# A two-layer encoder on one core: ten channel-major projections in half-width units with high and low part in one matmul, and memory in four parts

## What is computed

```python
h = rms_norm(x, mix_norm_g[i])
proj = h @ w_in[i]
da_q, da_k, da_v, s_z, s_xbc, s_dt, xa_q, gates = split_cols(proj, IN_SIZES)
y_da = diff_attention(da_q, da_k, da_v, lam, lambda_init, da_subln_g[i])
y_ssm = mamba2_bidir(s_z, s_xbc, s_dt, conv_w, conv_b, dt_bias, A_log, D, ssm_norm_g)   # convolution, silu, scans
y_xa = mem_cross_attention(xa_q, rms_norm(mem, mem_norm_g[i]), w_mem_kv[i])
x = x + (g0 * (y_da @ wb_da) + g1 * (y_ssm @ wb_ssm) + g2 * (y_xa @ wb_xa)) @ w_out[i]
gate, up = split_cols(rms_norm(x, ffn_norm_g[i]) @ w_ffn_in[i], (FFN_HIDDEN, FFN_HIDDEN))
x = x + (silu(gate) * up) @ w_ffn_out[i]
```

## Time and profile before

| what | value |
|---|---|
| median of 3 runs | 1413.91 us (1413.8 to 1414.85) |
| the profiled execution | 1414.03 us, its span 1412.3 us |
| TensorE busy | 1393.9 us (99%) |
| VectorE busy | 918.5 us (65%) |
| ScalarE busy | 885.6 us (63%) |
| GpSimd busy | 322.3 us (23%) |
| HBM traffic | 250.18 MB read, 178 GB/s over the span |

### The profile page before, as it was taken

How to read it: one execution, slowest core, us unless ns; L and a number is a source line. 1 busy time by engine, 2 the same in 40 slices (tenths; PEclk the granted TensorE clock), 3 DMA queues, 4 the chain that set the end, 5 groups by cost and what they waited for, 6 DMA issues and landing times.

```text
span 1412.3 us, 22092 instructions
## 1 busy us (share of the span) xinstructions
PE 1393.9 (99%) x8215; PEld 1222.1 (87%) x8231; DVE 918.5 (65%) x1243; ACT 885.6 (63%) x1432; POOL 322.3 (23%) x161
## 2 busy tenths in 40 slices
PE   7999999999999999999999999999999999999998
PEld 7899898888888889888899998988888888888886
DVE  5468575897998445554454775768889874555532
ACT  6576667986756446556445765778777464565543
POOL 0410000011023444444414000001110244344442
PEclk9999999999999999999999999999999999999999
DMA  7655445567665555666555555455756555566663
GB/s 250 189 172 174 124 134 166 159 199 200 203 194 178 183 177 180 192 192 218 185 184 170 165 152 147 133 174 143 223 190 230 179 166 192 164 194 182 192 194 119
DMA packets 157893, 252.80 MB, mean 179 GB/s; under 512 B 12649, under 2 KB 59355, under 8 KB 157787
## 3 DMA queue, kind: packets, MB, share of 16 engines
q1 hardware_dynamic: 156624, 249.50, 57.7%
q10 hardware_dynamic: 1163, 1.89, 0.4%
HBM read 250.18 MB, written 1.18 MB: 178 GB/s over the span
## 4 chain that ended last, share of the span: by engine, by line
PE 88%; DVE 4%; ACT 3%; DVEq 2%; DMA 1%; issue 1%; ACTq 0%; SPq 0%
PE PS L617 70%; PE S L617 14%; DVE wL L1367 1%; ACT wH L974 1%; PE S L624 1%; ACT scr L1135 1%; DVEq L1706 1%; DVE actLf L1635 1%; DMA w_raw<-in_w_in_dram 1%; DMA regA<-in_mem_dram 0%; PE S L936 0%; PE S L871 0%; DVEq L1637 0%; PE S L842 0%; DVE regA L1707 0%
## 5 line engine op out<-in xcount | busy, mean ns | idle before, releaser
L974 ACT CAST wH<-w_raw 128x1024 fp32r<-128x1024 f32 x440 | 457.6, 1043 | 457.4 <-PE PS L617 318.9
L1367 DVE TENSOR_TENSOR wL<-w_raw,wH 128x1024 fp32r<-128x1024 f32 (+1 forms) x328 | 416.0, 1273 | 341.9 <-ACT wH L974 323.3
L1302 POOL TENSOR_TENSOR wL<-w_raw,wH 128x1024 fp32r<-128x1024 f32 (+1 forms) x112 | 270.1, 2411 | 416.1 <-ACT wH L974 416.1
L617 PE MATMUL PS<-hHL,wH 128*128 128x256 f32 (+2 forms) x2016 | 314.8, 303 | 0.0
L617 PEld LDWEIGHTS PS<-hHL,wH 128*128 128x128 f32 (+1 forms) x2016 | 266.4, 190 | 10.9 <-issue 2.7
L617 PE MATMUL PS<-wH,actH 128*128 128x512 f32 x560 | 223.5, 399 | 0.0
L617 PE MATMUL PS<-wH,actL 128*128 128x512 f32 x560 | 218.4, 390 | 0.0
L617 PE MATMUL PS<-wH,hHL 128*128 128x512 f32 x768 | 200.7, 403 | 0.0
L617 PE MATMUL PS<-hHL,wL 128*128 128x256 f32 (+1 forms) x1168 | 172.0, 282 | 0.0
L617 PEld LDWEIGHTS PS<-wH,hHL 128*128 128x128 f32 x768 | 140.1, 188 | 33.3 <-issue 6.5
L617 PEld LDWEIGHTS PS<-hHL,wL 128*128 128x128 f32 (+1 forms) x1168 | 158.4, 190 | 6.2
(11 more groups left out here) (252 smaller groups left out, 1573.9 us busy)
## 6 DMA issues: line engine op xcount, KB each, us to landing
w_raw<-in_w_in_dram SPq DMA_DIRECT2D x192, 512.0 KB
w_raw<-in_w_ffn_in_dram SPq DMA_DIRECT2D x176, 256.0 KB
w_raw<-in_w_branch_dram SPq DMA_DIRECT2D x64, 512.0 KB
w_raw<-in_w_ffn_out_dram SPq DMA_DIRECT2D x44, 512.0 KB
w_raw<-in_w_mem_kv_dram SPq DMA_DIRECT2D x32, 512.0 KB
regA<-cs_rows SPq DMA_DIRECT2D x64, 256.0 KB, 4.9
w_raw<-in_w_out_dram SPq DMA_DIRECT2D x16, 512.0 KB
regA<-in_mem_dram SPq DMA_DIRECT2D x2, 768.0 KB, 7.0
```

What stands on the lines that cost most here:

```text
L617: return nc.tensor.matmul(o, l, r, start=first, stop=last, skip_group_check=True)
L974: nc.scalar.copy(wH[:, slot].rearrange("p k c -> p (k c)")[:, q], raw[:, slot].rearrange("p k c -> p (k c)")[:, q]).then_inc(h_done[slot], 1)
L1302: nc.gpsimd.tensor_tensor(wL[:, slot].rearrange("p k c -> p (k c)")[:, q], raw[:, slot].rearrange("p k c -> p (k c)")[:, q], wH[:, slot].r ...
L1367: v.tensor_tensor(wL[:, slot].rearrange("p k c -> p (k c)")[:, q], raw[:, slot].rearrange("p k c -> p (k c)")[:, q], wH[:, slot].rearrange ...
```

## The change

Ten groups per layer (xbc4, xq0, xbc5, xq1, xbc0, q0, k0, xbc1, q1, k1) get a layout W. A unit of theirs is 4 K tiles by 256 columns, so two units fill one pair of banks with half of the group: 2 tiles of 128 channels, each 512 columns wide, high and low activations side by side. The high weights take 8 matmuls of 512 columns and the low weights 8 of 256. The two halves of a bank have to be added: ScalarE copies the low half out (`wide_corr`, 512 columns), and VectorE adds it to the high half (`wide_sum`, 512 columns), which frees the pair. Such a group is two fills of PSUM, two units each. For xbc groups the middle tap now reads from `cin` (`conv_mid`) after the sum.

Memory comes in four parts of 256 columns between the first weight loads. The third and fourth block are transposed just ahead of unit 1's and unit 2's matmuls. VectorE copies the transposed blocks into `keep`, SyncE stores them to DRAM, and layer 1 reads them back and needs no transpose or squares. Parameter loads go from ScalarE's queue to SyncE's, behind the loads of the first four units. In the last layer the last two `down` units finish the first 128 tokens ahead of the others. The last output-projection group is added to x ahead of the weight subtraction that stood before it.

```diff
+    return [(kind, b, n, "W" if (kind, b) in WIDE else layout) for kind, b, n, layout in g]
+
+
+WIDE = [("xbc", 4), ("xq", 0), ("xbc", 5), ("xq", 1), ("xbc", 0), ("q", 0), ("k", 0), ("xbc", 1), ("q", 1), ("k", 1)]
 GROUPS = layer_groups()
 FIRST_UNIT = [sum(x[2] for x in GROUPS[:i]) for i in range(len(GROUPS))]
 UNITS = sum(x[2] for x in GROUPS)
 NGROUPS = len(GROUPS)
 UNIT_GROUP = [i for i, x in enumerate(GROUPS) for _ in range(x[2])]
-assert UNITS % RING == 0 and NGROUPS % 2 == 0
+FILLS = [2 if x[3] == "W" else 1 for x in GROUPS]
+FIRST_FILL = [sum(FILLS[:i]) for i in range(NGROUPS)]
+LAYER_FILLS = sum(FILLS)
+PAIR = [n % 2 for n in FIRST_FILL]
...
+        if (kind, b) in WIDE:
+            for half in range(2):
+                n = 2 * WIDE.index((kind, b)) + half
+                put(FIRST_UNIT[g] + 2 * half + 2, "act", "wide_corr", n)
+                put(FIRST_UNIT[g] + 2 * half + 2, "dve", "wide_sum", n)
+                if kind == "xbc":
+                    put(FIRST_UNIT[g] + 2 * half + 3, "act", "conv_mid", n)
...
+    put(4, "pe", "par_turn")
+    put(5, "dve", "params")
+    put(6, "sp", "mem_keep")
...
-    put(u + 6, "act", "mem_stats")
     put(u + 7, "dve", "mem_rstd")
     for b in range(4):
-        put(u + 9 + 2 * b, "pe", "mem_turn", b)
         put(u + 10 + 2 * b, "act", "mem_high", b)
...
+            for u in range(LOOKAHEAD):
                 load(0, u)
+                load_mem(u + 1)
+            load(0, LOOKAHEAD)
+            sp.dma_start(prm[0:120, 0:DEPTH, :], conv_w.rearrange("l t (c q) -> (t c) l q", q=P)).then_inc(par_in, 16)
...
+                        sp.wait_ge(mem_stored, 16)
+                        sp.dma_start(memT, mem_rows).then_inc(mem_in[0], 16)
+                    elif kind == "mem_keep" and lay == 0:
+                        for b in range(4):
+                            sp.wait_ge(side_free[b], 2)
+                        sp.dma_start(mem_rows, keep).then_inc(mem_stored, 16)
...
-            for b in range(4):
-                mem_turn(None, b)
-            setup_side = list(side)
+            for b in range(2):
+                mem_turn(b)
+            setup_side = [1, 1, 1, 1]
...
+                if c == 0 and kind != "outb" or layout == "W" and c == 2:
+                    pe.wait_ge(psum_free[pair], lay * (LAYER_FILLS // 2) + fill // 2 + 1)
...
+                if lay == 0 and kind == "mk" and b == 0 and c in (1, 2):
+                    mem_turn(c + 1)
...
+                elif layout == "W":
+
+                    at = 4 * (c % 2)
+                    w_h, w_l = (w[:, slot].rearrange("p k c -> p (k c)").rearrange("p (k c) -> p k c", k=4)
+                                for w in (wH, wL))
+                    for m in range(2):
+                        for kk in range(4):
+                            mm(dst[:, 2 * T * m:2 * T * (m + 1)], w_h[:, kk, P * m:P * (m + 1)], hHL[:, at + kk, :, :],
+                               c % 2 == 0 and kk == 0, False)
+                    pe.wait_ge(l_done[slot], use(lay, u) + 2)
+                    for m in range(2):
+                        for kk in range(4):
+                            ins = mm(dst[:, 2 * T * m:2 * T * m + T], w_l[:, kk, P * m:P * (m + 1)], hH[:, at + kk, :],
+                                     False, c % 2 == 1 and kk == 3)
...
-                    for t in range(NT):
+
+                    def rows(t, c):
+                        slot = (FIRST_UNIT[g] + c) % RING
                         for kk in range(UT):
                             k = a0 + UT * c + kk
                             a_h, a_l = aH_[:, k, P * t:P * (t + 1)], aL_[:, k, P * t:P * (t + 1)]
                             o = dst[:, UC * t:UC * (t + 1)]
                             mm(o, a_h, wH[:, slot, kk, :], False, False)
                             mm(o, a_l, wH[:, slot, kk, :], False, False)
-                            ins = mm(o, a_h, wL[:, slot, kk, :], False, kk == UT - 1)
-                        if t == 0:
-                            ins.then_inc(down_half, 1)
+                            ins = mm(o, a_h, wL[:, slot, kk, :], False, c == units - 1 and kk == UT - 1)
+                        return ins
+
+                    ins = rows(0, c)
+                    if last_unit:
+                        ins.then_inc(down_half, 1)
+                        rows(1, c - 1)
...
-                if kind in ("xq", "q", "k"):
-                    wait_full(act, lay, g)
-                    dst = xqT[:, 4 * b:4 * b + 4, :] if kind == "xq" else (qT if kind == "q" else kT)[b]
-                    nc.scalar.copy(dst, v3(src[:, :], 4)).then_inc(psum_free[pair], 1)
-                elif kind == "v":
...
+                if kind == "wide_corr":
+                    g, half = GI[WIDE[i // 2]], i % 2
+                    pair = (PAIR[g] + half) % 2
+                    wait_full(act, lay, g, half)
+                    nc.scalar.copy(v3(corr[pair], 2), halves(PS[pair][:, :])[:, :, 1, :]).then_inc(wide_corr, 1)
+                elif kind == "conv_mid":
+                    b, half = WIDE[i // 2][1], i % 2
+                    act.wait_ge(wide_done, 2 * len(WIDE) * lay + i + 1)
+                    for j in range(2 * half, 2 * half + 2):
+                        t = 4 * b + j
+                        q = CONV_T * 2 + t
+                        ins = nc.scalar.activation(conv_tile(CONV_ORDER.index(b))[:, j, :], cin[:, j, 2:2 + T], ACT.Identity,
+                                                   bias=p_cb[:, t:t + 1], scale=p_cw[:, q:q + 1])
+                    ins.then_inc(conv_mid, 1)
...
+            nc.scalar.activation(xsum[:, 0:1], eps, ACT.Copy, scale=eps)
+            act.wait_ge(psum_free[1], 1)
             for b in range(4):
-                mem_high(None, b, gmem[:, 0:8])
+                act.wait_ge(mem_turned, b + 1)
+                mem_high(lambda k: S[b][:, T * k:T * (k + 1)], b, gmem[:, 0:8])
                 if b < 3:
...
+                elif kind == "wide_sum":
+                    (what, b), half = WIDE[i // 2], i % 2
+                    g = GI[what, b]
+                    pair = (PAIR[g] + half) % 2
+                    q = slice(2 * half, 2 * half + 2)
+                    if what == "xq":
+                        if lay == 0 and b == 0:
+                            dve.wait_ge(mem_stored, 16)
+                        dst = xqT[:, 4 * b:4 * b + 4, :][:, q]
+                    elif what == "xbc":
+                        dst = cin[:, q, 2:2 + T]
+                    else:
+                        dst = (qT if what == "q" else kT)[b][:, q]
+                    dve.wait_ge(wide_corr, 2 * len(WIDE) * lay + i + 1)
+                    v.tensor_tensor(dst, halves(PS[pair][:, :])[:, :, 0, :], v3(corr[pair], 2), ALU.add
+                                    ).then_inc(psum_free[pair], 1)
+                    dve.drain().then_inc(wide_done, 1)
...
+                    if ("xbc", b) in WIDE:
+                        dve.wait_ge(conv_mid, 8 * lay + 2 * n + i % 4 // 2 + 1)
+                    elif i % 4 == 0:
...
+                v.tensor_copy(keep[:, 2 * b:2 * b + 2, :], v3(S[b][:, :], 2)).then_inc(side_free[b], 1)
...
+                    if u == LAST_OUT:
+                        evac(lay, g)
```

More of the change, by code:

```diff
@@ L402, in build @@
         par_in, row_in, x_in, stored = (sem(n) for n in ("par_in", "row_in", "x_in", "stored"))
-        mem_in = [sem(f"mem_in{part}") for part in range(2)]
-        gain_in, gain_turned, gain_ready = (sem("mem_gain_" + n) for n in ("in", "turned", "ready"))
+        mem_in = [sem(f"mem_in{part}") for part in range(4)]
+        mem_stored = sem("mem_stored")
+        gain_in, gain_turned = sem("mem_gain_in"), sem("mem_gain_turned")
         raw_in = [sem(f"raw_in{s}") for s in range(RING)]
@@ L597, in step, with unit @@
                                      ).then_inc(rowb_in[i % len(RB)], 16)
-                each_step("sp", lambda u, g, c: load(lay, u + LOOKAHEAD), lambda g: None, lambda *s: step(lay, *s))
+                def unit(u, g, c):
+                    if lay or u:
+                        load(lay, u + LOOKAHEAD)
+                each_step("sp", unit, lambda g: None, lambda *s: step(lay, *s))
             sp.wait_ge(hid_ready, N_FFN * DEPTH)
@@ L679, in unit @@
                 kind, b, units, layout = GROUPS[g]
-                slot, pair = u % RING, g % 2
+                fill = FIRST_FILL[g] + (c // 2 if layout == "W" else 0)
+                slot, pair = u % RING, fill % 2
                 if kind == "ffn" and b in (1, 2) and c == 0:
@@ L1419, in evac @@
                 kind, b = GROUPS[g][:2]
-                pair = g % 2
+                pair = PAIR[g]
                 src = PS[pair]
```

144 lines of the change are left out of this document (68 added, 76 removed).

## The result

The changed kernel takes 1439.13 us (median of 5 runs, 1438.61 to 1440.77) against 1413.94 (1413.8 to 1414.85) of the kernel before: ratio 1.0179, 95% interval 1.0168 to 1.0191. That is slower, as forecast, but by 25.2 us and not by 14.5: outside the range. The profiled execution took 1440.77 us, with a span of 1439.0.

The account below looks back on a forecast made before the run. The prediction took TensorE, busy 99% of the span, as the bound. Waits net of layout W's gain 15.4, start 2.1, less 1.8 (memory) and 1.2 (x), made 14.5 us more: 1428.5 us, range 1417 to 1437.

Parts of the forecast that it names:

- The clock falls at the start: Rival: TensorE's clock falls after 5 us idle ahead of unit 3, adding 1.5 us, 1430.0 us; chance 0.2.
- Matmuls of layout W: W units take 2.80 us instead of 2.88, 0.08 less each over 40 units and 2 layers: 6.4 us less.
- Unit 26: TensorE waits 1.9 us in each layer for VectorE's sum of xq0's first half.
- Unit 28: TensorE waits 1.2 us in each layer for VectorE's sum of xq0's second half.
- Unit 34: TensorE waits about 1.7 us ahead of this unit in each layer.
- Scores: First head's cross scores wait some 4.5 us for VectorE's sum of xq1's second half, starting 8.1 us later.
- Unit 52: Its fill waits 0.7 us per layer for the pair of banks until ScalarE has copied v0 out.
- Later backlog: Units 55 to 61: xbc1's convolution steps meet five sums on VectorE; 0.8 us waiting per layer, bounds 0 and 3.
- The start: Unit 3 starts at 24.05 us against 21.98, behind memory block 3's turning and ScalarE's chain: 2.1 us more.
- Memory for layer 1: Four blocks of transposes leave TensorE in layer 1: 1.8 us less.
- x added ahead: Adding x ahead of the weight subtraction removes a 0.6 us wait of transposes in each layer: 1.2 us less.
- The rival that the sums hide: Every sum comes before its pair of banks is wanted, so TensorE never waits: 1406.7 us, faster; chance 0.10.

Follow-up runs that it names:

- e5: Changed kernel plus spare 512-column matmuls on TensorE ahead of its waits at units 26, 34, the first cross scores, and unit 3 of layer 0: 1431.43 us.
- e13: Changed kernel, all ten groups wide, with ScalarE's decay step and the two small VectorE steps waiting for it eight units later: 1430.68 us.
- e7: Changed kernel with xq 0, xq 1, q 1, k 1 back in layout T, and weight block 3 cast ahead of scaling memory block 3: 1408.76 us.
- e11: Changed kernel, but GpSimd instead of VectorE subtracts the odd weight blocks up to block 37 (before: up to 25): 1446.25 us.
- e2: Changed kernel with only xq 0 and xq 1 back in layout T with ScalarE's evacuation, eight groups wide: 1415.15 us.
- e16: As e13, with two sums (first half of xq 0, second half of xq 1) one unit earlier: 1424.23 us.
- e12: Changed kernel with xq 1 and k 1 back in layout T, eight groups wide including xq 0: 1421.02 us.
- e6: Changed kernel with weight block 3 cast ahead of scaling memory block 3, and subtracted ahead of VectorE's wait for the root: 1435.1 us.

## Why the prediction missed

Direction and mechanism held, the size did not. The step that failed is the clock. The sum took each of its own waits at its bare length, and the fall of the clock stood only in the rival *The clock falls at the start*: at one place, worth 1.5 us, with a chance of 0.2, beside the remark that "no row of before shows a fall after full speed". The trace of the changed kernel shows the fall behind both waits of 2 us or more in each layer and behind the one at the start, and e5 prices it: 7.7 us by the medians. That is most of the 10.7 by which 25.2 exceeds 14.5: with the clock kept, e5's 1431.4 us lies inside the range of 1417 to 1437. By the traces it is 8.3: 2.3 at unit 3, and 3.0 in each layer. In a layer unit 26 gives 1.55, less 1.3 that unit 28 then waits, plus 1.3 for the wait of unit 32 that is not there, plus 1.6 at the scores. No row of before could show the fall, as TensorE hardly waits there behind its start. But the prediction itself put idle times of 1.9 and 4.5 us into each layer, and had a row of half clock behind 3.97 us of idle.

Step by step:

- *Matmuls of layout W*: 0.08 a unit forecast, 0.087 measured (2.79 against 2.88). The 7.5 ns a pair of its rows would have made only 0.06 of the 0.08; measured are 11 ns a pair. The 2.5 ns of the Trainium skill ("TensorE: Matmul & The Clock Gate", Wait — 56ns, not 53.3ns?) do not come out here either.
- *Unit 26*: 1.9 forecast, 2.07 measured, and 1.5 of half clock. *Unit 28*: 1.2 forecast, none measured, 1.1 in e5: the half clock at unit 26 gave VectorE the time. In its place unit 32 waited 1.2, which e5 does not have and e13 shows to hang on ScalarE's casts. *Unit 34*: 1.7 forecast, 1.87 measured in layer 0 and 1.48 in layer 1. *Scores*: 4.5 forecast, 3.90 measured, and 1.6 of half clock.
- *Unit 52*: 0.7 forecast, 0.57 measured. *Later backlog*: 0.8 taken, 1.65 of waiting and 1.8 from unit to unit measured, all of it ahead of attention turn 3, and ended by ScalarE, not by VectorE's sums. This is the second term that was too small, 1 us in each layer. e7, with q 1 and k 1 tall, does not have it.
- A layer so: 7.7 forecast, 12.4 and 12.2 measured.
- *The start*: +2.1 forecast, +6.2 measured, of which 2.3 is unit 3 at half clock. Unit 3 was forecast at 24.05; it stood at 25.54 in this execution and at 24.06 to 25.11 in the eleven other profiles with this start. ScalarE's chain from block 3's scaling to the cast of unit 3 took what was forecast; it began at 17.57 and not at 16.1. 0.4 of this is unit 0's later start (8.38 against 7.95), most of the rest is the clock once more: the forecast took over the 4.40 us that unit 0 took before, where its last part ran at full speed, but three us earlier all of it stood at half clock, 5.25 us. In e11, whose unit 3 stood at 24.06, the matmuls of unit 0 came to full pace at 10.7 us; here they did not before its end.
- *Memory for layer 1*: -1.8 forecast, -2.0 measured. *x added ahead*: -1.2 forecast, -1.4 measured. A wait of 0.6 before unit 109 in layer 0 went as well, which was not forecast.
- The rival that the sums hide named its condition as 9 us less ahead of the last sum. e2 and e16 bear the condition out in kind: the wait hangs on the place of the sum. That the eight other groups cost next to nothing once the cross queries are tall the prediction did not say.

What stays open: why attention turn 3 still waits 0.87 us with q 1 wide and k 1 tall. It was seen in both layers of one kernel (e12) and not taken apart. Open is also what e6's start gives with all ten groups tall.

## What to carry to other kernels

A stall of TensorE is to be priced twice: its length, and the half speed of the matmuls behind it where the clock falls, here 1.5 to 2.3 us for each. When PSUM's evacuation moves from one engine to another, ask group by group who wants the result soonest and what stands ahead on the new engine: without two groups of ten the whole loss was gone here. Then ask what the change gives by itself: six wide groups gave 2.2 us, and most of the fastest kernel's lead came from memory and x, with a start that cost 0.4 us and no longer 5.3. And where an engine lags, a result moved ahead in its order pushes the wait to the next one, so a fix is to be costed on the whole stretch.
